# Two groups of a gated feed-forward: products chained in PSUM pairs, the accumulator tile left out

## The chip, the cores and the metric

The kernel runs on one core of one Trainium2 chip. The time is that of one execution on the device, in microseconds (us), as the median of several runs. A profile is one execution recorded by the hardware profiler. Its engines are TensorE (PE, with its weight loads as PEld), VectorE (DVE), ScalarE (ACT), GpSimd (POOL) and SyncE (SP, which issues plain transfers).

## What is computed

Two transformer layers and then one convolution and attention block, all in float32, on 512 tokens of width 1024. The change touches only the last feed-forward:

```python
h = rms_norm_2(x, norm2_g[l])
u = causal_depthwise_conv(h @ w_up[l].astype(h.dtype), ffn_conv_w[l], ffn_conv_b[l])
u_val, u_gate = jnp.split(u, 2, axis=-1)
x = x + (jax.nn.silu(u_gate) * u_val) @ w_down[l].astype(x.dtype)
```

`w_up` is 1024 x 5632, `w_down` is 2816 x 1024; the hidden width 2816 is 22 chunks of 128.

## The kernel before

**Splitting.** Every float32 product is made of three on PE: each operand is cut into a high part and a low remainder, and high x high, low x high and high x low are added in PSUM. The weights come as units, blocks of 128 x 1024 values (512 KB). A unit goes through four hands: SP loads it (`load`), or for some units GpSimd adds a second block to it in place by an accumulating transfer (`g_seven`, L3020); ACT copies the high part into WH (`a_high`, L1299, mark `whi`); VectorE writes the remainder into WL (`v_low`, L2030, mark `wlo`); PE multiplies. WH and WL have four slots, so the high part of unit n waits until PE has finished unit n - 4. `a_cut(u)` and `v_cut(u)` cut all units up to u that are not cut yet, in order.

**The last feed-forward** (`t_ffn`, `v_ffn`, `a_ffn`) works in groups: 16 expansions (`fup0`; each one unit, 24 matmuls, an output of 128 x 512), then the products of those eight hidden chunks with `w_down` (`sevenf0`), then the same again (`fup1`, `sevenf1`), then 12 expansions and a shorter last group (`fup2`, `sevenf2`). The trace's group 0 and group 1 below are `sevenf0` and `sevenf1`.

**Seven products.** The product of a group is a 2 x 2 block product (2 token halves by 2 column halves of the output) done by Winograd's scheme with seven block products instead of eight. They are called b11, b21, t1, b22, t2, t3, t4. The hidden side of each is one of seven mixtures in AH and AL (`SIDE`). The weight side of b11, b21 and b22 is a plain block, that of t1, t2, t3, t4 a sum that GpSimd's transfers build up: t1's block is loaded and b12 added; t2's is t1's remainder block plus b22, in the same slot (the low part of t1 must have been cut: `sum_of = ("wlo", t1)`); t3 is loaded and added to; t4 comes from t2 likewise. Each product has two units, for h = 0 and 1, of 12 matmuls each: two token tiles (v, one PSUM bank each) x two chunks x three. So a group is 14 units, numbered 0 to 13 in the order of `STREAM`; "unit 7" in the prediction is the eighth.

**The output quadrants** are those of the residual X (`quarter_x(i, j)`), to which VectorE adds the products from their pair of PSUM banks once the unit for h = 1 is finished (`part`, L2929 for additions, L2931 for subtractions, L2927 for a copy). b11 also goes into an accumulator tile U2, together with t2, and over both groups; after group 1 U2 is added to or taken from three quadrants (`together`, L2941) during the next expansions.

**Orders.** Each engine's queue is in order. VectorE's in a group (`seven(o)` in `v_ffn`), at step j of 0 to 13, is: `v_cut(u + j + 3)`, at the first three steps the last hidden chunk's work, then the `part` of the product that ended with unit j - 1. PE waits at the first matmul of a product for its banks to be free (`k.free`), that is for the `part` of the product that had them. GpSimd's order of additions is `F_SUMS`. The expansions take their banks from a ring: 6, 7, 0, 1, 2, 3, 4, 5 after group 0, and 2, 3, 4, 5, 6, 7, 0, 1 after group 1. Raw weight blocks have seven slots (four in WR, three in MT); a load waits for the low part of the unit that had the slot, and SP issues the loads in the order of the units.

Of the kernel before, what the change touches and what calls it, by code (L numbers as in the profile page):

```python
# [144 lines left out]

def stream_of(name):

    return {"sevenf2": LAST_STREAM, "sevenv0": V_STREAM, "sevenw0": V_STREAM, "seveny0": Y_STREAM}.get(name, STREAM)


def plan(m, d):
# [109 lines left out]
def memory(nc):  # L261

    m = Memory()
# [24 lines left out]
    acc = at[0]  # L288
# [32 lines left out]
    m.RW = over("RW", [128, 2, 2, T], acc)  # L321
    m.SW = over("SW", [128, 2, 4, 256], acc + 8 * KB)
    m.SF = arena("SF", [128, 2, 4, 256], 56)
    m.U2 = arena("U2", [128, 2, 512], 64)

    m.Q = arena("Q", [128, 4, T], 0)
    m.KI = arena("KI", [128, 4, T], 8)
# [109 lines left out]
class Taps:  # L437
# [14 lines left out]
    def take(self, n):  # L452
# [22 lines left out]
GLA_O = (6, 7)  # L475
STREAM = [("b11", 0), ("b21", 0), ("t1", 0), ("b11", 1), ("b21", 1), ("t1", 1), ("b22", 0), ("b22", 1), ("t2", 0), ("t2", 1),
          ("t3", 0), ("t3", 1), ("t4", 0), ("t4", 1)]
LAST_HIDDEN = (7, 15, FC2 - 1)
LAST_STREAM = [("b11", 0), ("b21", 0), ("t1", 0), ("b22", 0), ("b11", 1), ("b21", 1), ("t1", 1), ("t2", 0), ("t2", 1), ("b22", 1),
               ("t3", 0), ("t3", 1), ("t4", 0), ("t4", 1)]  # L480
# [15 lines left out]
Y_BANKS = {"b11": 4, "b21": 6, "t1": 2, "t2": 4, "b22": 2, "t3": 4, "t4": 0}  # L496
V_DECAYS, V_TURNS = (1, 4, 7, 10), (3, 6, 9, 12)
SEVEN_BANKS = {"b11": 0, "b21": 2, "t1": 4, "b22": 6, "t2": 0, "t3": 2, "t4": 4}
FFN_PARTS = {"b11": (((0, 0), 1), ("u2", 1)), "b21": (((0, 0), 1),), "t1": (((0, 1), 1), ((1, 1), 1)), "b22": (((0, 1), 1),),
             "t2": (("u2", 1),), "t3": (((1, 0), 1), ((1, 1), -1)), "t4": (((1, 0), 1),)}  # L500
GLA_DS = ((2, 3), (4, 5))


# [441 lines left out]
def t_seven(e, k, key, o):  # L945

    m, name = k.m, f"seven{key}{o}"
    u, stream = k.at[name], stream_of(name)
    last = name == "sevenf2"

    def pairs(j, h, b, f, v, start, stop):

        x = k.units[u + j]
        n = x.n // 4
        for q in range(n):
            p, w = 2 * h + q, slice(512 * q, 512 * q + 512)
            xh, xl = m.AH[:, p, f, tile(v)], m.AL[:, p, f, tile(v)]
            e.wait_ge(*k.on("side", key, 4 * o + p, SIDE_PART[f]))
            e.matmul(m.ps[b + v], xh, x.wh[:, w], start=start and q == 0, stop=False, skip_group_check=last)  # L959
            e.matmul(m.ps[b + v], xl, x.wh[:, w], start=False, stop=False, skip_group_check=last)  # L960
            y = e.matmul(m.ps[b + v], xh, x.wl[:, w], start=False, stop=stop and q == n - 1, skip_group_check=last)  # L961
        return y

    for j, (what, h) in enumerate(stream):
        b, f = (LAST_BANKS if last else SEVEN_BANKS)[what], SIDE[what]
        e.wait_ge(*k.on("wlo", u + j))
        if last and what == "t4":
            if h == 0:
                continue
            for v in range(2):  # L970
                e.wait_ge(*k.on(*k.free[b + v]))
                pairs(j - 1, 0, b, f, v, True, False)
                y = pairs(j, 1, b, f, v, False, True)
                y.then_inc(*(k.mark("unit", u + j) if v else k.mark("front", what)))
            continue
        for v in range(2):
            if h == 0:
                e.wait_ge(*k.on(*k.free[b + v]))
            y = pairs(j, h, b, f, v, h == 0 and not (last and what in ("t2", "t3")), h == 1)
            if last and what == "t2" and h and v == 0:  # L980
                y.then_inc(*k.mark("front", what))
        y.then_inc(*k.mark("unit", u + j))
        if h == 1:
            for v in range(2):
                k.free[b + v] = ("part", key, o, what, v) if last and what == "t2" else ("part", key, o, what)
# [1881 lines left out]
def v_ffn(e, k):  # L2867
    m, at = k.m, k.at
    prior = {}

    def taps(j):

        i, g = j // 2, j % 2
        tmp = raw_hidden(m, i) if g else m.VAL[:, i % 2, :]
        for t in (1, 0):
            if t:
                e.wait_ge(*k.on("raised", j))
                e.wait_ge(*k.on("ae", f_unit(k, j)))
            else:
                e.wait_ge(*k.on("uc", j, 1))  # L2880
            e.scalar_tensor_tensor(tmp, m.UP[:, 2 * (i % 2) + g, t:t + T], par(m, "fcw", (i + FC2 * g) * 3 + t, 1), tmp,  # L2881
                                   A.mult, A.add).then_inc(*k.mark("uc", j, t))

    def gated(i):
        tmp = raw_hidden(m, i)
        e.wait_ge(*k.on("silu", i))
        e.tensor_tensor(tmp, tmp, m.VAL[:, i % 2, :], A.mult).then_inc(*k.mark("ug", i))  # L2887

    def others(p):
        v_mix(e, k, "f", p, ("ug", 2 * p), ("ug", 2 * p + 1))  # L2890
        v_side_b(e, k, "f", p)

    def ups(a, b):

        for j in range(a, b):
            n = j - a
            taps(j)
            v_cut(e, k, f_unit(k, j) + 4)
            if a == 32 and n in (1, 3, 5):
                together(n // 2)  # L2900
            if n > 1 and n % 2 == 0:
                gated(j // 2 - 1)
            if n > 2 and n % 2:
                if n % 4 == 3:
                    v_side_a(e, k, "f", (j - 3) // 4)
                    if n > 3:
                        v_side_s(e, k, "f", (j - 7) // 4)
                else:
                    others((j - 5) // 4)

    def quarter_x(i, j):
        return m.X[:, 2 * i:2 * i + 2, 512 * j:512 * j + 512]

    def part(o, what, vs=slice(0, 2)):

        u, b = at[f"sevenf{o}"] + stream_of(f"sevenf{o}").index((what, 1)), (LAST_BANKS if o == 2 else SEVEN_BANKS)[what]
        src = pair(m, b).rearrange("p (a f) -> p a f", a=2)[:, vs]
        if vs == 0:
            e.wait_ge(*k.on("front", what))
        else:  # L2920
            e.wait_ge(*k.on("unit", u))
        for to, sign in (LAST_PARTS if o == 2 else FFN_PARTS)[what]:
            acc = (m.U2[:, :, :] if to == "u2" else quarter_x(*to))[:, vs]
            if to in prior:
                e.wait_ge(*k.on("part", "f", *prior[to]))  # L2925
            if to == "u2" and not o and what == "b11":
                e.tensor_copy(acc, src).then_inc(*k.mark("part", "f", o, what, to))  # L2927
            elif sign > 0:
                e.tensor_tensor(acc, src, acc, A.add).then_inc(*k.mark("part", "f", o, what, to))  # L2929
            else:  # L2930
                e.tensor_tensor(acc, acc, src, A.subtract).then_inc(*k.mark("part", "f", o, what, to))  # L2931
            if vs in (0, 1):
                k.also("part", "f", o, what, vs)
            prior[to] = (o, what, to)
        k.also("part", "f", o, what)

    def together(n):

        acc, op = ((quarter_x(0, 1), A.subtract), (quarter_x(1, 0), A.add), (quarter_x(1, 1), A.subtract))[n]
        e.wait_ge(*k.on("part", "f", 1, "t4"))  # L2940
        e.tensor_tensor(acc, acc, m.U2[:, :, :], op).then_inc(*k.mark("part", "f", "u2", n))  # L2941
        prior[((0, 1), (1, 0), (1, 1))[n]] = ("u2", n)

    def seven(o):

        u, stream = at[f"sevenf{o}"], stream_of(f"sevenf{o}")
        for j in range(14):
            if o == 2 and j > 4:
                break
            v_cut(e, k, u + j + 3)  # L2950
            if j == 0:
                gated(LAST_HIDDEN[o])
            elif j == 1:
                others(LAST_HIDDEN[o] // 2)
            elif j == 2:
                v_side_s(e, k, "f", LAST_HIDDEN[o] // 2)
            if j and o < 2 and stream[j - 1][1]:
                part(o, stream[j - 1][0])
        if o < 2:
            part(o, "t4")  # L2960
            return
        part(o, "b11")
        part(o, "b21")
        v_cut(e, k, u + 10)
        part(o, "t2", 0)
        part(o, "t2", 1)
        v_cut(e, k, u + 13)
        part(o, "t1")
        part(o, "b22")
        part(o, "t3")  # L2970
        part(o, "t4", 0)
        part(o, "t4", 1)

    e.memset(m.UP[:, :, 0:2], 0.0).then_inc(*k.mark("pads", "ffn"))
    for o in range(3):
        ups(16 * o, min(16 * o + 16, 2 * FC2))
        seven(o)
# [34 lines left out]
def g_seven(e, k, key, o):  # L3012

    m, name = k.m, f"seven{key}{o}"
    u = k.at[name]
    for what in F_SUMS if key == "f" else M_SUMS:
        j = stream_of(name).index(what)
        x = k.units[u + j]
        e.wait_ge(*k.on(*x.sum_of))
        e.dma_start(raw(m, x.raw)[:, 0:128 * x.n], x.more, accum_op=A.add).then_inc(*k.mark(f"added{x.raw}", u + j, by=16))  # L3020
# [243 lines left out]
```

## Time and profile before

| | us |
|---|---|
| median of 3 runs | 1903.86 (1903.72 to 1904.85) |
| span of the profiled execution, first to last instruction | 1900.5 |
| PE busy | 1890.5 |
| DVE busy | 1339.4 |
| ACT busy | 985.3 |

The profile gives the profiled execution no time of its own beside its span; the median of the runs is 3.4 us above it. The busy time of an engine is the time in which at least one of its instructions ran. Matmuls are pipelined: a row gives each some 0.39 us, while the next one starts well before that.

### The profile page before, as it was taken

To read this page: it belongs to the slowest core of one execution; us is meant where nothing else is said; L and a number is where in the kernel's file an instruction comes from. 1 tells how busy PE (TensorE), PEld (TensorE's weight loads), DVE (VectorE), ACT (ScalarE), POOL (GpSimd) and SP (SyncE) were. 2 spreads that over 40 slices of the span, in tenths; PEclk is the share of its full clock that TensorE was granted. 3 is DMA by queue.
4 is the path that set the end of the run, shared out by engine and by line. 5 is a ranking of instruction groups with operands and counts; after the bars stand their busy time and mean duration, and the time that the engine had idled before them with its cause. 6 is when DMAs were issued, how large, how long until landed. Compare 5 with 4: busy or idle time off the path is not lost. (4 is left out here: it accounts for less than half of the span.)

```text
span 1900.5 us, 25399 instructions
## 1 busy us (share of the span) xinstructions
PE 1890.5 (99%) x9486; PEld 1555.8 (82%) x9486; DVE 1339.4 (70%) x1988; ACT 985.3 (52%) x1587; POOL 95.3 (5%) x114
## 2 busy tenths in 40 slices
PE   9999999999999999999999999999999999999999
PEld 8877888887888778888888988667788888888887
DVE  7656665656566766665566788998897867767867
ACT  5634464544546746454444435788445446545454
POOL 0100000101000000000100000000000000100101
PEclk9999999999999999999999999999999999999999
DMA  7632156757323114756752356222224634644735
GB/s 230 155 100 94 73 142 180 166 162 202 123 79 144 46 56 132 201 139 173 180 162 67 112 143 167 89 90 78 89 91 143 166 89 155 155 148 118 199 95 122
DMA packets 69676, 249.79 MB, mean 131 GB/s; under 512 B 7730, under 2 KB 7986, under 8 KB 68916
## 3 DMA queue, kind: packets, MB, share of 16 engines
q1 hardware_dynamic: 55728, 198.88, 31.0%
q0 software_dynamic: 13824, 49.29, 14.8%
q8 instruction: 77, 1.26, 0.3%
q14 instruction: 43, 0.35, 0.1%
q10 hardware_dynamic: 4, 0.00, 0.0%
HBM read 246.05 MB, written 2.10 MB: 131 GB/s over the span
## 5 line engine op out<-in xcount | busy, mean ns | idle before, releaser
L545 PE MATMUL ps<-HH,WH 128*128 128x512 f32 (+1 forms) x1696 | 626.2, 369 | 0.9 <-ACT AT L1736 0.9
L547 PE MATMUL ps<-HH,WL 128*128 128x512 f32 (+1 forms) x1696 | 621.2, 366 | 0.0
L546 PE MATMUL ps<-HL,WH 128*128 128x512 f32 (+1 forms) x1696 | 620.9, 366 | 0.0
L1299 ACT ACTIVATE WH<-WR 128x1024 fp32r<-128x1024 f32 x333 | 348.9, 1056 | 479.8 <-PE ps L547 315.3
L2030 DVE TENSOR_TENSOR WL<-WR,WH 128x1024 fp32r<-128x1024 f32 (+1 forms) x332 | 403.1, 1218 | 263.1 <-ACT WH L1299 262.4
L545 PEld LDWEIGHTS ps<-HH,WH 128*128 128x128 f32 x1696 | 319.9, 189 | 62.5 <-issue 11.6
L547 PEld LDWEIGHTS ps<-HH,WL 128*128 128x128 f32 x1696 | 319.9, 189 | 52.2
L546 PEld LDWEIGHTS ps<-HL,WH 128*128 128x128 f32 x1696 | 320.0, 189 | 50.7
L959 PE MATMUL ps<-WH,AH 128*128 128x512 f32 x490 | 191.0, 390 | 0.4 <-DVE WL L2030 0.4
L960 PE MATMUL ps<-WH,AL 128*128 128x512 f32 x490 | 190.7, 389 | 0.0
L961 PE MATMUL ps<-WL,AH 128*128 128x512 f32 x490 | 190.6, 389 | 0.0
L2576 DVE SCALAR_TENSOR_TENSOR M<-AP,PAR,M 128x512 f32<-128x512 f32 x240 | 166.1, 753 | 0.1
L959 PEld LDWEIGHTS ps<-WH,AH 128*128 128x128 f32 x490 | 92.0, 188 | 20.8 <-DVE WL L2030 1.7
L961 PEld LDWEIGHTS ps<-WL,AH 128*128 128x128 f32 x490 | 92.0, 188 | 19.0
L960 PEld LDWEIGHTS ps<-WH,AL 128*128 128x128 f32 x490 | 92.0, 188 | 19.0
L1919 ACT ACTIVATE UP<-ps 128x512 f32<-128x512 f32 x44 | 26.4, 599 | 116.5 <-PE ps L547 116.5
L3020 POOL DMA_DIRECT2D WR<-in_quart x48 | 41.8, 988 | 818.5 <-DMA WR<-in_quart 751.2
L2881 DVE SCALAR_TENSOR_TENSOR RW<-UP,PAR,RW 128x512 f32<-128x512 f32 x44 | 33.1, 752 | 43.3 <-ACT RW L1925 42.5
L2881 DVE SCALAR_TENSOR_TENSOR M<-UP,PAR,M 128x512 f32<-128x512 f32 x44 | 33.1, 752 | 37.7 <-ACT M L1925 36.9
L1307 ACT ACTIVATE HL<-X 128x1024 fp32r<-128x1024 f32 x24 | 25.4, 1060 | 34.8 <-DVE X L2091 24.4
L1318 ACT ACTIVATE HH<-ps 128x512 fp32r<-128x512 f32 x48 | 26.1, 594 | 31.2 <-PE ps L598 31.0
L1527 ACT ACTIVATE RW<-RW 128x512 f32<-128x512 f32 x64 | 40.6, 634 | 2.0
(386 smaller groups left out, 2606.9 us busy)
## 6 DMA issues: line engine op xcount, KB each, us to landing
WR<-in_up SPq DMA_DIRECT2D x96, 512.0 KB, 4.2
WR<-in_quart SPq DMA_DIRECT2D x60, 512.0 KB, 3.6
WR<-in_quart POOLq DMA_DIRECT2D x48, 512.0 KB, 6.3
WR<-in_in SPq DMA_DIRECT2D x48, 512.0 KB, 3.6
WR<-in_down SPq DMA_DIRECT2D x16, 512.0 KB, 3.5
WR<-in_quartf SPq DMA_DIRECT2D x14, 512.0 KB, 3.5
WR<-in_quartf POOLq DMA_DIRECT2D x14, 512.0 KB, 5.6
MT<-in_up SPq DMA_DIRECT2D x12, 512.0 KB, 4.1
```

Source lines behind the costliest of these rows:

```text
L545: e.matmul(ps, wh, hi[:, c, cols], start=c == 0, stop=False)
L546: e.matmul(ps, wh, lo[:, c, cols], start=False, stop=False)
L547: y = e.matmul(ps, wl, hi[:, c, cols], start=False, stop=c == x.n - 1)
L959: e.matmul(m.ps[b + v], xh, x.wh[:, w], start=start and q == 0, stop=False, skip_group_check=last)
L960: e.matmul(m.ps[b + v], xl, x.wh[:, w], start=False, stop=False, skip_group_check=last)
L961: y = e.matmul(m.ps[b + v], xh, x.wl[:, w], start=False, stop=stop and q == n - 1, skip_group_check=last)
L1299: e.activation(x.wh[:, 0:n], raw(m, x.raw)[:, 0:n], AF.Copy).then_inc(*k.mark("whi", u))
L1527: e.activation(buf, buf, AF.Square).then_inc(*k.mark("sqr", u))
L2030: e.tensor_tensor(x.wl[:, 0:n], raw(m, x.raw)[:, 0:n], x.wh[:, 0:n].bitcast(F32), A.subtract).then_inc(*k.mark("wlo", u))
L2576: e.scalar_tensor_tensor(m.M[:, c, :], m.AP[:, c, t:t + T], par(m, "conv_w", c * 31 + t, 1), m.M[:, c, :], A.mult, A.add).then_inc(*k.mark ...
L2881: e.scalar_tensor_tensor(tmp, m.UP[:, 2 * (i % 2) + g, t:t + T], par(m, "fcw", (i + FC2 * g) * 3 + t, 1), tmp, A.mult, A.add).then_inc(*k. ...
L3020: e.dma_start(raw(m, x.raw)[:, 0:128 * x.n], x.more, accum_op=A.add).then_inc(*k.mark(f"added{x.raw}", u + j, by=16))
```

## The change

For `sevenf0` and `sevenf1` alone the products are left in PSUM and continued: t2 is accumulated onto b11 in banks 0 and 1 (no `start`), t3 onto both; b22 onto t1 in banks 4 and 5; t4 has banks 2 and 3 after b21. VectorE reads a pair after each product and adds what it holds by then into a quadrant; with the signs of `CHAIN_PARTS` this gives the same four sums. U2, its copy and `together` go. The order of the units becomes that of `CHAIN_STREAM`: t2 is at 6 and 7, b22 at 8 and 9. GpSimd's order for these two groups is that of `M_SUMS`, in which t2 for h = 1 stands ahead of both t3.

```diff
@@ def stream_of(name)
-    return {"sevenf2": LAST_STREAM, "sevenv0": V_STREAM, ...
+    return {"sevenf0": CHAIN_STREAM, "sevenf1": CHAIN_STREAM, "sevenf2": LAST_STREAM, "sevenv0": V_STREAM, ...
@@ def memory(nc)
-    m.U2 = arena("U2", [128, 2, 512], 64)
@@
 STREAM = [("b11", 0), ("b21", 0), ("t1", 0), ("b11", 1), ("b21", 1), ("t1", 1), ("b22", 0), ("b22", 1), ("t2", 0), ("t2", 1),
           ("t3", 0), ("t3", 1), ("t4", 0), ("t4", 1)]
+CHAIN_STREAM = STREAM[:6] + [("t2", 0), ("t2", 1), ("b22", 0), ("b22", 1)] + STREAM[10:]
@@
 SEVEN_BANKS = {"b11": 0, "b21": 2, "t1": 4, "b22": 6, "t2": 0, "t3": 2, "t4": 4}
-FFN_PARTS = {"b11": (((0, 0), 1), ("u2", 1)), "b21": (((0, 0), 1),), "t1": (((0, 1), 1), ((1, 1), 1)), "b22": (((0, 1), 1),),
-             "t2": (("u2", 1),), "t3": (((1, 0), 1), ((1, 1), -1)), "t4": (((1, 0), 1),)}
+CHAIN_BANKS = {"b11": 0, "b21": 2, "t1": 4, "b22": 4, "t2": 0, "t3": 0, "t4": 2}
+CHAIN_STARTS = ("b11", "b21", "t1", "t4")
+CHAIN_PARTS = {"b11": (((0, 0), 1),), "b21": (((0, 0), 1),), "t1": (((1, 1), 1),), "t2": (((0, 1), -1),), "b22": (((0, 1), 1),),
+               "t3": (((1, 1), -1), ((1, 0), 1)), "t4": (((1, 0), 1),)}
@@ def t_seven(e, k, key, o)
-    last = name == "sevenf2"
+    last, chained = name == "sevenf2", name in ("sevenf0", "sevenf1")
...
-        b, f = (LAST_BANKS if last else SEVEN_BANKS)[what], SIDE[what]
+        b, f = (LAST_BANKS if last else CHAIN_BANKS if chained else SEVEN_BANKS)[what], SIDE[what]
...
-            y = pairs(j, h, b, f, v, h == 0 and not (last and what in ("t2", "t3")), h == 1)
+            y = pairs(j, h, b, f, v, h == 0 and not (last and what in ("t2", "t3")) and not (chained and what not in CHAIN_STARTS), h == 1)
@@ def v_ffn(e, k), ups
-            if a == 32 and n in (1, 3, 5):
-                together(n // 2)
@@ def v_ffn(e, k), part
-        for to, sign in (LAST_PARTS if o == 2 else FFN_PARTS)[what]:
-            acc = (m.U2[:, :, :] if to == "u2" else quarter_x(*to))[:, vs]
+        for to, sign in (LAST_PARTS if o == 2 else CHAIN_PARTS)[what]:
+            acc = quarter_x(*to)[:, vs]
...
-            if to == "u2" and not o and what == "b11":
-                e.tensor_copy(acc, src).then_inc(*k.mark("part", "f", o, what, to))
-            elif sign > 0:
+            if sign > 0:
@@ def v_ffn(e, k)
-    def together(n):
-
-        acc, op = ((quarter_x(0, 1), A.subtract), (quarter_x(1, 0), A.add), (quarter_x(1, 1), A.subtract))[n]
-        e.wait_ge(*k.on("part", "f", 1, "t4"))
-        e.tensor_tensor(acc, acc, m.U2[:, :, :], op).then_inc(*k.mark("part", "f", "u2", n))
-        prior[((0, 1), (1, 0), (1, 1))[n]] = ("u2", n)
@@ def g_seven(e, k, key, o)
-    for what in F_SUMS if key == "f" else M_SUMS:
+    for what in F_SUMS if name == "sevenf2" else M_SUMS:
```

## Rows read from the trace of the kernel before

**Rows 1.** The page: busy us of each engine, share of the span, instructions.
```profile
PE 1890.5 (99%) x9486; PEld 1555.8 (82%) x9486; DVE 1339.4 (70%) x1988; ACT 985.3 (52%) x1587; POOL 95.3 (5%) x114
```

**Rows 2.** Waits of PE, whole span: us in total, times, longest.
```profile
PE ps L884 <- DVE DG L2981: 1.2, 1, 1.2
...
PE ps L959 <- DVE WL L2030: 0.4, 2, 0.2
```

**Rows 3.** Busy us by stage: PE, PEld, DVE, ACT, POOL, clock, DMA share, GB/s.
```profile
1638.90:1677.00 38.10, 38.10 (x170) 31.56 (x169) 32.60 (x33) 17.97 (x20) 4.31 (x5) 1.00 0.86 213
...
1764.00:1802.00 38.00, 38.00 (x169) 31.48 (x168) 32.58 (x33) 18.31 (x20) 4.33 (x5) 1.00 0.86 219
```

**Rows 4.** Timeline of PE: start us, length us, line, operation, tiles.
```profile
1638.89 0.39 PE L959 MATMUL ps<-WH,AH 128*128 128x512 f32 x1
...
1764.01 0.39 PE L959 MATMUL ps<-WH,AH 128*128 128x512 f32 x1
...
1801.87 0.39 PE L961 MATMUL ps<-WL,AH 128*128 128x512 f32 x1
1802.09 0.39 PE L545 MATMUL ps<-HH,WH 128*128 128x512 f32 x1
...
1895.71 0.39 PE L961 MATMUL ps<-WL,AH 128*128 128x512 f32 x1
```

**Rows 5.** Groups of instructions, 1500 to 1901: busy, mean ns, idle before.
```profile
L2941 DVE TENSOR_TENSOR X<-X,U 128x1024 f32<-128x1024 f32 x3 | 3.7, 1219 | 0.0
```

**Rows 6.** Timeline of DVE in group 0; in brackets the idle time before.
```profile
1648.39 1.22 DVE L2030 TENSOR_TENSOR WL<-WR,WH 128x1024 fp32r<-128x1024 f32 x1
...
1651.79 1.22 DVE L2030 TENSOR_TENSOR WL<-MT,WH 128x1024 fp32r<-128x1024 f32 x1
1652.93 1.21 DVE L2929 TENSOR_TENSOR X<-ps,X 128x1024 f32<-128x1024 f32 x1
1654.06 1.21 DVE L2927 COPY U<-ps 128x1024 f32<-128x1024 f32 x1
...
1660.98 1.23 DVE L2030 TENSOR_TENSOR WL<-WR,WH 128x1024 fp32r<-128x1024 f32 x1 [3.44 <-ACT WH L1299]
```

**Rows 7.** Timeline of DVE in group 1.
```profile
1773.50 1.22 DVE L2030 TENSOR_TENSOR WL<-WR,WH 128x1024 fp32r<-128x1024 f32 x1
...
1802.54 1.22 DVE L2929 TENSOR_TENSOR X<-ps,X 128x1024 f32<-128x1024 f32 x1
```

**Rows 8.** Timeline of POOL, first feed-forward, then groups 0 and 1: accumulating transfers.
```profile
453.22 0.86 POOL L3020 DMA_DIRECT2D WR<-in_quart  x1 [10.38 <-DMA WR<-in_quart]
...
1648.94 1.82 POOL L3020 DMA_DIRECT2D WR<-in_quartf  x2 [9.20 <-DMA WR<-in_quartf]
...
1775.02 0.86 POOL L3020 DMA_DIRECT2D WR<-in_quartf  x1 [1.14 <-DVE WL L2030]
```

**Rows 9.** Line 3020: all; at 453.2; at 454.3 to 455.4; at 1775.0.
```profile
DMA to landing us min/median/max: 4.0/6.1/12.3
...
DMA to landing us min/median/max: 5.5/5.5/5.5
...
L3020 POOL DMA_DIRECT2D WR<-in_quart x3: 865/1219/1571, 454.3 to 455.4; - x3
DMA to landing us min/median/max: 7.4/9.4/12.3
...
DMA to landing us min/median/max: 7.1/7.1/7.1
```

**Rows 10.** Timelines of ACT, DVE and PE, first feed-forward, group 2.
```profile
458.73 1.06 ACT L1299 ACTIVATE WH<-WR 128x1024 fp32r<-128x1024 f32 x1 [4.88 <-DMA WR<-in_quart]
...
459.82 1.22 DVE L2030 TENSOR_TENSOR WL<-WR,WH 128x1024 fp32r<-128x1024 f32 x1 [3.58 <-ACT WH L1299]
...
461.10 0.50 PE L959 MATMUL ps<-WH,AH 128*128 128x512 f32 x1 [0.18 <-DVE WL L2030]
```

**Rows 11.** Timeline of ACT in group 1: a high part waits for PE.
```profile
1791.47 1.06 ACT L1299 ACTIVATE WH<-WR 128x1024 fp32r<-128x1024 f32 x1 [1.66 <-PE ps L961]
```

More of the change, by code:

```diff
@@ L146, in stream_of @@
 def stream_of(name):
-    return {"sevenf2": LAST_STREAM, "sevenv0": V_STREAM, "sevenw0": V_STREAM, "seveny0": Y_STREAM}.get(name, STREAM)
+    return {"sevenf0": CHAIN_STREAM, "sevenf1": CHAIN_STREAM, "sevenf2": LAST_STREAM, "sevenv0": V_STREAM, "sevenw0": V_STREAM, "seveny0": Y_STREAM}.get(name, STREAM)
 def plan(m, d):
@@ L958, in pairs @@
             e.wait_ge(*k.on("side", key, 4 * o + p, SIDE_PART[f]))
-            e.matmul(m.ps[b + v], xh, x.wh[:, w], start=start and q == 0, stop=False, skip_group_check=last)
-            e.matmul(m.ps[b + v], xl, x.wh[:, w], start=False, stop=False, skip_group_check=last)
-            y = e.matmul(m.ps[b + v], xh, x.wl[:, w], start=False, stop=stop and q == n - 1, skip_group_check=last)
+            e.matmul(m.ps[b + v], xh, x.wh[:, w], start=start and q == 0, stop=False, skip_group_check=last or chained)
+            e.matmul(m.ps[b + v], xl, x.wh[:, w], start=False, stop=False, skip_group_check=last or chained)
+            y = e.matmul(m.ps[b + v], xh, x.wl[:, w], start=False, stop=stop and q == n - 1, skip_group_check=last or chained)
         return y
     for j, (what, h) in enumerate(stream):
-        b, f = (LAST_BANKS if last else SEVEN_BANKS)[what], SIDE[what]
+        b, f = (LAST_BANKS if last else CHAIN_BANKS if chained else SEVEN_BANKS)[what], SIDE[what]
         e.wait_ge(*k.on("wlo", u + j))
@@ L2914, in part @@
     def part(o, what, vs=slice(0, 2)):
-        u, b = at[f"sevenf{o}"] + stream_of(f"sevenf{o}").index((what, 1)), (LAST_BANKS if o == 2 else SEVEN_BANKS)[what]
+        u, b = at[f"sevenf{o}"] + stream_of(f"sevenf{o}").index((what, 1)), (LAST_BANKS if o == 2 else CHAIN_BANKS)[what]
         src = pair(m, b).rearrange("p (a f) -> p a f", a=2)[:, vs]
```

## The prediction

> **What bounds the kernel now.** The page comes first. Its busy shares [rows 1] put PE at 1890.5 us of a span of 1900.5 and DVE at 1339.4: the reader is to see that PE has 10.0 us without work in the whole program, so that anything taken from another engine can win only out of those 10. The waits of PE over the whole span [rows 2] show how small its stops are: the longest is 1.2 us, at the start, and all that its seven groups of waits give to VectorE's low halves is 0.4 us. Then the busy times by stage [rows 3]: in group 0 of the last feed-forward (1638.9 to 1677) PE is busy for all of 38.10 us, in group 1 for all of 38.00, at a granted clock of 1.00 (of 2.4 GHz). DVE has 32.6 us of work in each: 5.5 us idle. Last the matmuls themselves [rows 4]: group 1's first starts at 1764.01 and its last, the 168th, at 1801.87, so 0.2267 us from one to the next, and the first expansion of the next stage starts at 1802.09, again in step. A unit (one weight block, 12 matmuls) is 2.72 us. The last matmul of the program starts at 1895.71; the other 4.8 us are the final additions and the output. PE is without a gap through all of this, so each us by which a matmul of these groups is late is added to the end, and nothing given back to DVE alone is a gain.
>
> **What is removed.** VectorE's sums for these two groups go from 10 to 8 instructions each (b11 and t1 had two targets, now one), and the three additions of the accumulator go: seven instructions. The three cost 3.7 us [rows 5], one of the others is the copy at 1654.06 [rows 6]; in the queue each takes 1.14 us, the distance of two starts in [rows 6], together 8.0 us. They lie beside PE, which waits for none of them, so I cost the removal at nothing. If that cover were gone, 8.0 us is what it could bring.
>
> **What is moved.** t2 goes from units 8 and 9 to 6 and 7, before b22, since it now piles onto b11's banks 0 and 1. Two orders change with it.
>
> PE: unit 6 (t2, h 0) must wait until VectorE has read b11 out of banks 0 and 1. Before, banks 0 and 1 were wanted again only at unit 8.
>
> VectorE: its queue is in order. At step 4 of a group it first makes the low half of unit 7, then adds b11. Before, unit 7 was b22, a plain load: low half at 1651.79, b11 at 1652.93 [rows 6]. Now unit 7 is t2 for h 1, whose weights are a sum: t1's block must be cut by VectorE (unit 5), then GpSimd's accumulating transfer adds b22 to it in place, then ACT cuts the high half, then VectorE the low one. The trace of before already shows this chain as a wait: VectorE stood 3.44 us before the low half at 1660.98 [rows 6]. There, nobody wanted what stood behind it in the queue. Now b11's addition stands behind it, and PE waits for that.
>
> **The cost, group 0.** Unit 6 is due 72 matmuls after 1638.89: at 1655.21. The low half of unit 5 starts at 1648.39 and takes 1.22 [rows 6], so 1649.61. GpSimd's start follows by 0.30: in group 1 the same low half ends at 1773.50 + 1.22 = 1774.72 [rows 7] and the transfer is issued at 1775.02 [rows 8]. So 1649.91, which is when the second of the two at 1648.94 went out too [rows 8]. Its landing is the disputed price. GpSimd's new order puts t2 for h 1 ahead of both t3, so it is the first of a burst. The nearest row is that of the first feed-forward at 453.22 [rows 8]: issued 1.1 us ahead of three more, landed after 5.5 [rows 9]. I take 5.5. It gives 1655.41. From landing to ACT's start 0.01 (453.22 + 5.5 against 458.73, [rows 8, 10]), from there to the low half 1.09, [rows 10]; to the next instruction, b11's addition, 1.14; its length 1.21 [rows 6]; from VectorE's end to the matmul 0.06 (459.82 + 1.22 against 461.10, [rows 10]). Sum: 1655.41 + 0.01 + 1.09 + 1.14 + 1.21 + 0.06 = 1658.92, late by 3.71. The first matmul after such a stop takes 0.50 instead of 0.39 [rows 10], 0.11 more: **3.8 us**.
>
> **Group 1.** Unit 6 is due at 1764.01 + 72 x 0.2267 = 1780.33. 1775.02 + 5.5 + 3.51 = 1784.03, late by 3.70, with the restart **3.8 us**. In general the stall is the landing time less 1.7.
>
> **Bounds of the landing.** From below, the fastest of all accumulating transfers, 4.0 [rows 9]: 2.3 us a group. From above, what this transfer took in group 1, as second of its burst, 7.1 [rows 9]: 5.4 us a group. The slowest of all, 12.3 (10.6 us), was the last of a burst of three; this one is first.
>
> **Behind the stall.** In group 0, PE resumes at 1658.92 and wants banks 4 and 5 for b22 at 1664.36. VectorE's queue after b11 (start 1657.65): low of unit 8, b21, low of unit 9, then t1's single addition at 1662.2, done 1663.4: 0.9 us in hand. The next reuse is t3 on banks 0 and 1 at 1669.8, wanting t2's addition. That stands behind the low half of unit 11, whose high half needs unit 7 finished plus 0.26 (ACT starts 0.26 after a unit's end: 1791.47 in [rows 11] against 1764.01 + 120 x 0.2267 = 1791.21), so 1664.6, + 1.09 + 1.14 + 1.21 = 1668.1: 1.7 us in hand. The transfers for t3 follow the first landing at about 3 us each: three issued within 1.1 us landed after 7.4 to 12.3 [rows 9]. That puts them near 1658.5 and 1661.6, in time. t4's two have until unit 12, 8 us later. These I cost at nothing. On SP's queue the loads for the second and third expansion now wait for the low halves of units 8 and 9 instead of 6 and 7; their blocks are wanted at units 15 and 16, over 13 us after that, more than the slowest landing of [rows 9], so nothing either. All the later steps hang on PE's progress and shift with it.
>
> **The end of group 1.** t4 moves from banks 4 and 5 to 2 and 3, and the expansions that follow group 1 take bank 2 first. Their first matmul, at 1802.09 in [rows 4], now waits for t4's addition, the last instruction of the group. In the row it runs 1802.54 + 1.22 = 1803.76 [rows 7]; + 0.06, late by 1.73, with the restart **1.8 us**. This one is well bounded: the same instruction, the same place in the queue. After group 0 the expansions begin at banks 6 and 7, which no product of the chained group uses: nothing there.
>
> **Sum:** 3.82 + 3.81 + 1.84 = +9.5 us. On the profiled execution that is 1900.5 to 1910.0 of span. The page gives that execution no other time; the median of the runs, 1903.86, lies 3.4 us above its span, so 1913.3.
>
> **The clock.** Nothing here shows what a stop of 3.7 us does to it: the only stops in [rows 2] are up to 1.2 us, and the granted clock is 1.00 in both stages of [rows 3]. The Trainium skill speaks against this change there (TensorE: Matmul & The Clock Gate, HAM oscillation): waits that leave PE idle for long between stretches of matmuls throttle its clock again, each time. No row here shows a stop of such a length. By the rows the sum is +9.5; by the page a slow stretch follows both stops, which is the second rival, +14.9.
>
> **Rivals.**
> 1. Forecast, two stalls behind b11 and one behind t4, 1910.4 to 1916.5: 72 in 100. For it: program order alone makes them.
> 2. The granted clock falls to its lower level (1.2 GHz) after each of the two long stops, for about one unit: 2.72 us more each, +14.9, 1918.8. Against it: clock 1.00 in all rows, also behind the short stops. 7 in 100. The Trainium skill's rule above would make this the normal case.
> 3. A second wait in each group: the transfers for t3 come late, behind one another and the loads. They have about 3 us before hi of unit 11 wants them and 1.7 more before PE stops; a landing 6 us later than I have it costs 1.3 a group, 1916 in all, one of 3 us a group would make 1919. 10 in 100.
> 4. The long stalls don't appear, since the first transfer lands early: the stall is gone at 1.7 us of landing. Only the t4 wait is left, +1.8, 1905.7. Against it: the minimum is 4.0. Counting in that the order of VectorE's queue is misread, 8 in 100.
> 5. The other side: PE's matmul times hold hidden waits for VectorE, and seven instructions fewer bring 7 x 1.14 = 8.0 us, 1895.9. It decides if PE anywhere in [rows 3] stood for VectorE, against which the even step of 0.2267 speaks. 3 in 100.
>
> **The numbers.** Within 0.2% (3.8 us) is about what a measurement of this kernel can't tell from no change. Faster: 0.03 (rival 5). Same: 0.08 (rival 4). Slower: 0.89. The range takes the forecast's bounds, 2 x 2.3 + 1.84 = +6.5 (1910.4) to 2 x 5.4 + 1.84 = +12.7 (1916.5), down to 1909.5 for one stall smaller, and up to 1918.5 for most of rival 3.
>
> **What would show it.** In the profile after: PE waiting on line 959 twice for VectorE's addition into X, about 3.6 us each at the seventh unit of groups 0 and 1, and once about 1.6 us on line 545 at the first expansion after group 1. VectorE idle some 4 to 5 us before the low half of unit 7, right before b11's addition. 16 additions into X from PSUM in these two groups, no instruction on U. GpSimd's t2 for h 1 issued before both t3 and landing after 5 to 6 us. The granted clock at 1.00. Wrong would be: a landing under 3 us, b11's addition ahead of the low half of unit 7, or a gap of PE anywhere else.

## The result, and the profile after

| | before | changed |
|---|---|---|
| median, us | 1903.72 (5 runs) | 1916.41 (1913.21 to 1917.29, 5 runs) |
| span of the profiled execution | 1900.5 | 1914.5 |
| mean granted clock over the span | 1.00 | 0.997 |

The ratio is 1.0064, 95% interval 1.0052 to 1.0076: slower, by 12.7 us between the medians and 14.0 between the spans. The two differ because the kernel before was profiled in one of its faster executions: wherever both are on record for one execution, the time is 1.8 to 2.4 us above the span, not 3.4. The value forecast was 1913.3, in a range of 1909.5 to 1918.5.

In the changed kernel the lines of the file move by some numbers: 2032 is the low half, 2927 an addition into X, 2929 a subtraction, 1301 the high half, 961 to 963 the matmuls of the groups, 547 an expansion's, 3011 the accumulating transfer. The page's busy shares, against [rows 1]:

```profile
PE 1894.8 (99%) x9486; PEld 1557.9 (81%) x9486; DVE 1332.3 (70%) x1981; ACT 984.6 (51%) x1587; POOL 95.3 (5%) x114
```

VectorE has its seven instructions and 7.1 us less; PE, with the same 9486 matmuls, is busy for 4.3 us more. So the work did not only get gaps, some of it became slower. The waits of PE over the span (us in total, times, longest), against [rows 2]:

```profile
PE ps L961 <- issue: 6.9, 2, 3.5
PE ps L547 <- DVE X L2927: 1.7, 1, 1.7
...
PE ps L961 <- DVE WL L2032: 1.2, 2, 0.6
```

Three are new: two of 3.5 and 3.4 us on line 961 and one of 1.7 on line 547. The last row is the wait for low halves, 0.4 us in [rows 2]. It lies in the first feed-forward and varies from one execution to the next; unit 5 of group 0 ends when it did before (last matmul at 1654.92, before at 1654.98 by the step of [rows 4]), so it is no part of the change. The view puts the first two down to "issue", that is to nothing that it can name; what they waited for has to be read from VectorE's timeline. PE's timeline at the first of them, where unit 6 of group 0 begins:

```profile
1654.92 0.39 PE L963 MATMUL ps<-WL,AH 128*128 128x512 f32 x1
1658.83 0.77 PE L961 MATMUL ps<-WH,AH 128*128 128x512 f32 x1 [3.52 <-issue]
1659.39 0.63 PE L962 MATMUL ps<-WH,AL 128*128 128x512 f32 x1
1659.82 0.63 PE L963 MATMUL ps<-WL,AH 128*128 128x512 f32 x1
...
1664.84 0.39 PE L963 MATMUL ps<-WL,AH 128*128 128x512 f32 x1
1665.07 0.39 PE L961 MATMUL ps<-WH,AH 128*128 128x512 f32 x1
```

And VectorE's and GpSimd's timelines at the same place, against [rows 6] and [rows 8]:

```profile
1649.83 0.86 POOL L3011 DMA_DIRECT2D WR<-in_quartf  x1 [11.04 <-DVE WL L2032]
```

```profile
1648.32 1.22 DVE L2032 TENSOR_TENSOR WL<-WR,WH 128x1024 fp32r<-128x1024 f32 x1
...
1650.59 1.22 DVE L2032 TENSOR_TENSOR WL<-MT,WH 128x1024 fp32r<-128x1024 f32 x1
1656.37 1.22 DVE L2032 TENSOR_TENSOR WL<-WR,WH 128x1024 fp32r<-128x1024 f32 x1 [4.56 <-ACT WH L1301]
1657.51 1.22 DVE L2927 TENSOR_TENSOR X<-ps,X 128x1024 f32<-128x1024 f32 x1
```

The chain is there link by link: the low half of unit 5 ends at 1649.54, GpSimd issues the transfer that completes t2's weights at 1649.83, it lands 5.4 us later, VectorE stands 4.56 us until ACT has made the high half, makes the low half of unit 7 at 1656.37, adds b11 from 1657.51 to 1658.73, and PE's unit 6 starts at 1658.83.

One thing more differs from the forecast, the step between matmuls after the stop: 0.43 us instead of 0.2267. Busy times by stretch (the columns of [rows 3]; the last but two is the granted clock) show what that is:

```profile
1654.90:1658.80 3.90, 0.41 (x2) 0.00 (x1) 2.43 (x3) 2.95 (x3) 0.86 (x1) 0.88 1.01 199
1659.40:1664.50 5.10, 5.10 (x13) 3.96 (x12) 3.86 (x4) 0.12 (x1) 0.00 (x0) 0.50 1.06 217
1665.10:1681.00 15.90, 15.90 (x72) 13.15 (x71) 10.03 (x9) 5.65 (x7) 0.00 (x0) 1.00 0.67 222
...
1784.00:1790.00 6.00, 2.98 (x14) 2.13 (x12) 2.07 (x2) 2.95 (x3) 1.59 (x3) 1.00 1.04 197
```

From 1659.4 to 1664.5 the granted clock is 0.50, the lower of its two levels (1.2 GHz), then 1.00 again. Before it fell, PE had done nothing for up to 3.52 us: the first row, the stop itself, has 0.88, so the fall came in the last part of the stop. In group 1 it came later still: the clock is 1.00 over the stop (last row) and up to 1791.0, when PE had been at work again for 0.6 us, and 0.50 from there to 1794.3. The account of the span, each lateness being the step less 0.2267 us:

| | late, us |
|---|---|
| stop before unit 6, group 0 (1654.92 to 1658.83) | 3.68 |
| 14 steps behind it (to 1664.84) | 2.84 |
| stop before unit 6, group 1 (1786.59 to 1790.39) | 3.57 |
| 11 steps behind it (to 1794.57) | 1.69 |
| stop behind t4 (1813.62 to 1815.66) | 1.81 |
| one step behind it | 0.08 |
| sum | 13.67 of 14.0 |

PE's last matmul is 13.7 us later than before; the other 0.3 us come after it.

### The profile page after: what moved, and what is told of

It is laid out like the page before. It is cut to its first block and busy times, and to the rows that moved or that the text cites. A ratio compares the mean times of both kernels' runs of the same rounds, so it can differ in the third digit from the quotient of the medians.

```text
span 1914.5 us, 25392 instructions
## 1 busy us (share of the span) xinstructions
PE 1894.8 (99%) x9486; PEld 1557.9 (81%) x9486; DVE 1332.3 (70%) x1981; ACT 984.6 (51%) x1587; POOL 95.3 (5%) x114
## 5 line engine op out<-in xcount | busy, mean ns | idle before, releaser
L547 PEld LDWEIGHTS ps<-HH,WH 128*128 128x128 f32 x1696 | 319.8, 189 | 64.1 <-issue 13.7
```

The lines of the kernel that those rows point to most:

```text
L547: e.matmul(ps, wh, hi[:, c, cols], start=c == 0, stop=False)
```

## The experiments

Each kernel was timed beside the kernel before on the same chip. Its median there was 1903.27 for e1 to e4 (15 runs) and 1903.87 for e5 to e8 (7 runs).

**e1: b11's addition ahead of the low half of unit 7**

```diff
@@ def seven(o), changed kernel
+            if j == 4 and o < 2:
+                part(o, "b11")
             v_cut(e, k, u + j + 3)
...
-            if j and o < 2 and stream[j - 1][1]:
+            if j > 4 and o < 2 and stream[j - 1][1]:
                 part(o, stream[j - 1][0])
```

> The changed kernel, with b11's addition ahead of the low half of unit 7 in VectorE's queue, in both groups; all else as changed. Queue theory: both stops of 3.6 us at unit 6 go, and with them the stretch at the lower clock (2.8 and 1.7 us). The low half of unit 7 still comes at about 17.6 us into the group and t1's addition stands three instructions behind it, so PE should stop some 1.6 us before unit 8 instead (t1's banks), plus 1.8 us behind t4: about 1903.7 + 2 x 1.6 + 1.8 = 1908.7. Rival (the stop belongs to taking banks 0 and 1 again two units sooner, whatever the order): PE still stops at unit 6 and the time stays near 1916.

Measured 1909.79 us (4 runs), ratio 1.0035 (1.0021 to 1.0049), granted clock 1.00 in every run. PE's waits in each half of the last feed-forward:

```profile
PE ps L961 <- issue: 1.6, 1, 1.6
...
PE ps L961 <- issue: 1.5, 1, 1.5
PE ps L547 <- DVE X L2927: 1.7, 1, 1.7
```

The stops at unit 6 are gone. In their place PE stops two units later, for t1's addition:

```profile
1663.53 0.39 PE L963 MATMUL ps<-WL,AH 128*128 128x512 f32 x1
1665.48 0.47 PE L961 MATMUL ps<-WH,AH 128*128 128x512 f32 x1 [1.56 <-issue]
```

It resumes as VectorE's addition at 1664.16 + 1.22 ends. One position in VectorE's queue is the cause of both long stops; the rival, that reusing the banks early costs by itself, is out. The span, 1909.2, is 8.7 us above that of the kernel before, more than the three stops: 3.1 us of it were lost before this feed-forward, in waits for low halves that the edit doesn't touch. The three stops with a step behind each are 5.4 us; the medians differ by 6.5.

**e2: the expansions after group 1 begin at banks 4 and 5**

```diff
@@ def t_ffn(e, k), changed kernel
-    k.ring(2, 3, 4, 5, 6, 7, 0, 1)
+    k.ring(4, 5, 6, 7, 0, 1, 2, 3)
     ups(at["fup2"], 0, 12)
```

> The changed kernel, with the expansions after group 1 beginning at banks 4 and 5 (4, 5, 6, 7, 0, 1, 2, 3) instead of 2 and 3. Theory: only the stop of 1.65 us behind t4 goes, 1916.4 - 1.8 = 1914.6; the two stops in the groups stay. Rival (VectorE is late as a whole at the end of group 1, so the wait moves to the next expansion's bank): no gain.

Measured 1913.90 us (4 runs), ratio 1.0059 (1.0045 to 1.0073). The wait on line 547 for X is gone, those on line 961 are 3.5 and 3.5 us. In its trace the step from group 1 into the expansion is even:

```profile
1812.26 0.39 PE L963 MATMUL ps<-WL,AH 128*128 128x512 f32 x1
1812.49 0.39 PE L547 MATMUL ps<-HH,WH 128*128 128x512 f32 x1
```

So the third stop was the choice of a bank. It is the trace that shows this. The median is 2.5 us below the changed kernel's where 1.8 was expected, but the spread of either's runs, 2.9 and 4.1 us, is larger than that, and the slow steps in this trace cost 1.68 and 1.42 us, 1.4 less than in the changed kernel's.

**e3: b11, b21 and t1 ahead of unit 7, and e2's banks**

```diff
@@ def seven(o), changed kernel with e2's ring
+            if j == 4 and o < 2:
+                for what in ("b11", "b21", "t1"):
+                    part(o, what)
             v_cut(e, k, u + j + 3)
...
-            if j and o < 2 and stream[j - 1][1]:
+            if j > 6 and o < 2 and stream[j - 1][1]:
                 part(o, stream[j - 1][0])
```

> The changed kernel, with b11's, b21's and t1's additions all ahead of the low half of unit 7 in VectorE's queue, and the expansions after group 1 beginning at banks 4 and 5. Queue theory: no stop of PE is left in these groups, the granted clock is 1.00 throughout, and the time is that of the kernel before, 1903.7, within 1 us; the seven instructions fewer bring nothing. Rival (VectorE's 8 us count): up to 8 us faster than before. Rival (chaining costs in itself): slower than before by 4 us or more.

Measured 1903.68 us (11 runs), ratio 1.0000 (0.9991 to 1.0009). The same stages as in [rows 3]:

```profile
1638.90:1677.00 38.10, 38.10 (x169) 31.44 (x168) 31.67 (x32) 17.07 (x19) 4.41 (x5) 1.00 0.82 219
...
1764.00:1802.00 38.00, 38.00 (x170) 31.37 (x169) 31.53 (x32) 17.18 (x19) 4.41 (x5) 1.00 0.84 220
```

PE is full again and the clock is 1.00. Within the interval, 1.7 us either way, the chaining costs nothing; neither does it bring anything, with seven instructions and an accumulator tile (4 KB of each partition) fewer. Both rivals, 8 us faster and 4 us slower, are out. This is the best form of the change that was tried, and it is equal to the kernel before.

**e4 and e7: matmuls whose results nobody reads, inside the stop**

```diff
@@ def t_seven(e, k, key, o), changed kernel; 14 in e4, 5 in e7
+        if chained and j == 6:
+            e.wait_ge(*k.on(*k.free[6]))
+            for _ in range(14):
+                e.matmul(m.ps[6], m.HH[:, 0, 0:128], m.HH[:, 1, :], start=True, stop=True)
         for v in range(2):
```

> The changed kernel, with 14 more matmuls (high half of the hidden input by itself, into the unused bank 6, not read by anyone) ahead of the wait of unit 6 in both groups: 14 x 0.227 = 3.2 us of PE's work inside a stop of 3.7. Clock theory: the stop itself stays, PE resumes at the same time, but PE is idle for only 0.4 us, the granted clock stays at 1.00, and the 2.8 and 1.7 us behind the stops are saved: about 1916.4 - 4.5 = 1911.9. Rival (the slow matmuls come from something else in unit 6, such as adding onto a bank that VectorE has read): step 0.43 us as before, no gain.

Measured 1912.38 us (4 runs), ratio 1.0048 (1.0035 to 1.0062). PE's timeline at the two stops:

```profile
1654.47 3.33 PE L981 MATMUL ps<-HH 128*128 128x512 f32 x14
1658.21 0.50 PE L961 MATMUL ps<-WH,AH 128*128 128x512 f32 x1 [0.40 <-DVE X L2931]
1658.54 0.39 PE L962 MATMUL ps<-WH,AL 128*128 128x512 f32 x1
...
1783.46 3.33 PE L981 MATMUL ps<-HH 128*128 128x512 f32 x14
1788.15 0.50 PE L961 MATMUL ps<-WH,AH 128*128 128x512 f32 x1 [1.36 <-DVE X L2931]
```

From the last matmul of unit 5 (1654.25) to unit 6 it is still 3.96 us, and behind it the steps are 0.33 once and 0.23 from then on: the stop unchanged, the slow stretch gone. The clock was 1.00 over 1658.2 to 1664.0 and behind group 1's stop too. That stop was longer here, 4.92 us from 1783.23 to 1788.15, because its transfer took 6.5 us; PE was idle for 1.36 of it. 1916.41 - 1912.38 = 4.0 us (3.6 if each is set against the kernel before beside it), against the 4.5 (2.84 + 1.69) that the slow steps took in the profile of the changed kernel. So it is the idle time that brings the lower clock, and not something in unit 6. This also gives the wait a name, where the view had said "issue": the addition into X (line 2931 in this kernel).

> The changed kernel, with 5 more matmuls into the unused bank 6 ahead of the wait of unit 6: 1.1 us of work, then 2.5 us idle instead of 3.6. Clock theory: what PE does without work decides, so the stretch at the lower clock is shorter or absent in some executions; between 1911.9 (no fall of the clock) and 1916.4. Rival: no change.

Measured 1915.35 us (1912.23 to 1916.07, 4 runs). In the profiled execution, the fastest of the four, PE stood for 2.4 and 2.6 us and the clock stayed at 1.00:

```profile
1655.19 1.29 PE L981 MATMUL ps<-HH 128*128 128x512 f32 x5
1658.92 0.50 PE L961 MATMUL ps<-WH,AH 128*128 128x512 f32 x1 [2.44 <-DVE X L2931]
```

The others can be read from the mean granted clock of their spans. It is 1.000 here (span 1910.4) and 0.999, 0.998 and 0.998 in the others (spans 1912.7, 1913.5 and 1914.2). No run of e1, e3, e4 or the kernel before has less than 0.999; those of the changed kernel have 0.997 or 0.998. So the clock very probably fell in at least two of the four executions, behind stops that five matmuls were to cut to 2.5 us of idle time. How long PE stood in just those executions is not on record. This is the "shorter or absent in some executions" that was expected: five matmuls are not enough to be sure of the clock.

**e5: the order alone, on the kernel before**

```diff
@@ kernel before: STREAM and F_SUMS for groups 0 and 1 only; banks, U2, together kept
-    return {"sevenf2": LAST_STREAM, ...
+    return {"sevenf0": CHAIN_STREAM, "sevenf1": CHAIN_STREAM, "sevenf2": LAST_STREAM, ...
...
-    for what in F_SUMS if key == "f" else M_SUMS:
+    for what in F_SUMS if name == "sevenf2" else M_SUMS:
```

> The kernel before (its own banks, U2 and its three additions all kept), with only the order of the units and of GpSimd's additions in groups 0 and 1 taken from the change. In the kernel before, t2 has banks 0 and 1 as well, so it waits for b11 too, and b11 has two instructions there. Queue theory: PE stops before unit 6 for 3.6 + 1.1 = 4.8 us in each group, and the clock falls behind it (about 2 us each): 1903.7 + 9.6 + 4 = 1917, with no stop behind t4. Rival (the stops belong to the chained accumulation): as before, 1903.7.

Measured 1919.21 us (4 runs), ratio 1.0079 (1.0064 to 1.0094): more than the changed kernel, without a chained product, and 2 us more than expected. The rival, chained accumulation, is out. PE's waits by half:

```profile
PE ps L960 <- issue: 4.6, 1, 4.6
...
PE ps L960 <- issue: 4.9, 1, 4.9
```

The waits are 1.1 and 1.5 us longer than the changed kernel's 3.5 and 3.4. b11's second instruction makes 1.1 of each, as expected; the other 0.4 in group 1 is the transfer, 5.7 us instead of 5.3. VectorE's timeline has the second instruction between the first and PE's start at 1660.62:

```profile
1657.03 1.22 DVE L2031 TENSOR_TENSOR WL<-WR,WH 128x1024 fp32r<-128x1024 f32 x1 [4.46 <-ACT WH L1300]
1658.17 1.22 DVE L2930 TENSOR_TENSOR X<-ps,X 128x1024 f32<-128x1024 f32 x1
1659.30 1.22 DVE L2928 COPY U<-ps 128x1024 f32<-128x1024 f32 x1
```

**e6: GpSimd's order of before, in the changed kernel**

```diff
@@ def g_seven(e, k, key, o), changed kernel
-    for what in F_SUMS if name == "sevenf2" else M_SUMS:
+    for what in F_SUMS if key == "f" else M_SUMS:
```

> The changed kernel, with GpSimd's additions for groups 0 and 1 in the order of before: t2 for h = 1 behind both t3. Queue theory, stop = landing of that sum less 1.7 us: the landing was 10.0 us in group 0 and 7.1 us in group 1 in the trace of before, so stops of 8.3 and 5.4 us instead of 3.6 and 3.6, 6.5 us more, and a stretch at the lower clock of at least the same length: 1923 or more. Rival (the landing doesn't matter): 1916.4.

Measured 1920.53 us (4 runs), ratio 1.0083 (1.0067 to 1.0100). The direction held, the size didn't: the stops make PE late by 5.18 and 4.51 us, not 8.3 and 5.4. The landings were 6.9 and 6.2 us (line 3011, the two issued at 1651.0 and 1652.0, and the one at 1784.0):

```profile
DMA to landing us min/median/max: 5.4/6.1/6.9
...
DMA to landing us min/median/max: 6.2/6.2/6.2
```

6.9 - 1.7 = 5.2 and 6.2 - 1.7 = 4.5: the formula is right within 0.1 us, its input was not. In the trace of before two loads for expansions were issued during this transfer; with t2 ahead of b22 their slots come free two units later, so they are out of its way. That this is why it landed sooner was not tried.

**e8: the changed kernel once more**

> The changed kernel once more, one look: the two stops before unit 6 at 3.5 us within 0.3, the stop behind t4 at 1.65, and the stretch of the lower clock of another length than 2.8 and 1.7 us, if where it begins and ends is a matter of chance; the span differs from 1914.5 by just the difference of those lengths.

1917.69 us (one run), span 1915.9. PE stood for 4.1 and 3.8 us, the first outside the 0.3 expected, the second just within (late by 4.23 and 3.93), and 1.7 behind t4. The landings were 6.0 and 5.7 us: again landing less 1.7, 4.3 and 4.0. The slow steps behind cost 1.68 and 2.98 us, against 2.84 and 1.69 in the first profile. Their sum is nearly the same, so the expectation that the spans would differ by just these lengths failed: of the 1.4 us between the spans, 0.9 is the longer stops and 0.5 was there before this feed-forward. Both the landing and the slow stretch vary from one execution to the next. How much of the 4.1 us over which the changed kernel's runs spread is theirs is not shown: the kernel before has neither, and its 15 runs beside e1 to e4 spread over 4.4 us.

## Why the prediction was right, and where it was short

- **What bounds the kernel**, and nothing for the removal: right. e3 has the seven instructions fewer, and its ratio is 1.0000 (0.9991 to 1.0009).
- **The stop before unit 6**: right in place, cause and size. Expected late by 3.71 and 3.70 without the restart, measured 3.68 and 3.57; landing 5.5 taken, 5.4 and 5.3 measured. In the changed kernel, its repeat, e2 and e6 the lateness is the landing less 1.75 us each time, for landings of 5.3 to 6.9. e1 (remove it), e5 (it alone) and e6 (another landing) tie it to VectorE's queue behind the sum for t2.
- **Behind the stall**: no other stop, right, in e4 too, where no slow stretch gave VectorE more time. The transfers for t3 were put near 1658.5 and 1661.6 and landed at 1658.9 and 1661.4. e1 tests the same working with the stop lifted: 1.6 us expected at unit 8, 1.56 and 1.48 measured.
- **The end of group 1**: 1.73 expected, 1.81 measured; e2 removes it.
- **The restart**: too small a term. The first matmul after the stop was costed at 0.11 us, from stops of 0.2 us idle. That is about right for the stops of up to 2.6 us in the profiles of e1, e4, e7 and behind t4 (0.08 to 0.11). Behind the two long ones it was 2.84 and 1.69, 4.5 us where 0.22 was taken.
- **The clock** is that term's cause, and the step that failed: rival 2 was given 7 in 100 "against it: clock 1.00 in all rows", but no row had a stop of that length, so the rows were no evidence either way. "The granted clock at 1.00", listed among what would show the forecast, did not come. Rival 2 priced 2.72 us for each stop; measured 2.84 and 1.69, by e4 worth 3.6 to 4.0 us together. By spans the account closes: 1910.0 was forecast and 1914.5 measured, 4.5 short, and the steps behind the three stops took 4.61 where the sum had 0.33. The Trainium skill (TensorE: Matmul & The Clock Gate, HAM oscillation) had said that such waits throttle the clock again; the trace agrees, with a granted clock of 0.50 from 1659.4 to 1664.5.

The value was therefore 3.1 us low, with the right sign. That it lay inside the range was in this part luck: the range had been carried up to 1918.5 for rival 3's sake, and rival 3 did not happen, while rival 2, which did, stood at 1918.8, outside it. What happened is the forecast's three stops and rival 2 together.

## What to carry to other kernels

When a product is moved up in the order, go through every in-order queue for what now stands ahead of the instruction that frees its buffer: a wait that cost nothing (3.44 us of VectorE in [rows 6]) becomes PE's as soon as something wanted stands behind it. An addition that frees PSUM belongs ahead of a preparation that may wait for a transfer; moving three additions up and beginning the next stage at banks that nobody is still reading brought the time back to that of the kernel before. Price a stop of PE together with the clock that follows it: if no stop of that length is in the trace, the trace says nothing about the restart.

## What the runs showed of the hardware

In these profiles PE stood ten times for 3.4 us or more before unit 6 with nothing to do (3.4 to 5.0 us, twice each in the changed kernel, its repeat, e2, e5 and e6). Behind each of them 7 to 15 steps between matmuls were slow, 0.43 us instead of 0.23 and up to 0.57 for the first, 1.4 to 3.0 us lost; over 1659.4 to 1664.5 in the changed kernel, wholly within such a stretch, the granted clock read 0.50. None of the profiled stops of 1.4 to 2.6 us (e1, e4, e7, and the one behind t4) was followed by this. That is not shown to be a safe length: by the mean clocks of e7's other runs it very probably fell in two of them, where 2.5 us of idle time were planned.

The length of the slow stretch did not follow that of the stop: in one execution 4.1 us idle cost 1.68, and 3.8 us cost 2.98. Nor did the clock always fall while PE stood: in group 1 of the changed kernel it fell 0.6 us after PE had resumed, in group 0 of e8 0.4 us after (1.00 over 1659.9 to 1660.3, 0.50 over 1660.4 to 1663.7).
